# The low-part products of a sublayer's first two weight blocks, tile by tile for both blocks

## The chip, the cores and the metric

The kernel runs on one core of a Trainium2 chip. The metric is the device time of one execution, in microseconds. Before the change the median of three executions is 2408.03 us (2402.39 to 2408.96). About 0.3%, 7.2 us, is what a measurement of this kernel can tell from no change.

## The reference, cut to what matters

Two layers (DEPTH = 2) act on 544 token columns: 512 of a new stream and 32 of a running one. A layer is a half-step SwiGLU network, a mixer (latent attention beside retention) and a second half-step SwiGLU network, three sublayers in all:

```
h = modulated_pre(x, norm_pre[l, 0], mods, 0)      # rms_norm(x, g) * (1 + scale) + shift
x = gated_post(x, swiglu(h, w1, w3, w2), norm_post[l, 0], mods, 0, 0.5)
h = modulated_pre(x, norm_pre[l, 1], mods, 1)
o, st = mixer(h, l)                                # begins with z = h @ w_in
x = gated_post(x, o, norm_post[l, 1], mods, 1, 1.0)
h = modulated_pre(x, norm_pre[l, 2], mods, 2)
x = gated_post(x, swiglu(h, ...), norm_post[l, 2], mods, 2, 0.5)
```

Everything is float32. The model width is 1024 (8 tiles of 128 features), the hidden width 2816.

## The kernel before, in words

Activations lie feature-major: `x[:, k, :]` holds features 128k to 128k+127 on the partitions and the 544 tokens along the free axis. A matrix product in float32 accuracy is made of three products in the faster fp32r type: each operand is split into a high part (rounded to fp32r) and a low part (what is left), and high x high, high x low and low x high are added up in PSUM. `tile3` (L583, L584, L587) does this for one 128x128 weight tile, in two halves of the tokens.

Weights are streamed in chunks: a chunk is the column of 8 weight tiles that makes one output tile. SyncE loads chunk c into `raw[:, c % 2]`, ScalarE rounds it into `w_hi` (`high`, L1029, or `high_at`, L1036), GpSimd writes the rest into `w_lo` (`low`, L486), and TensorE multiplies. There are two slots of each. `high` of chunk c+2 waits on the semaphore `w_used` until TensorE has used chunk c, since both lie in one slot; `low` of c+2 waits for `high` of c+2, and TensorE's next block waits for `lo_done` of its chunk.

The change is in `first_tiles`, which makes the first two output tiles of each sublayer, chunks 0 and 1 (`w` = 0, 1) together, because the input h is only being made at that time. It runs six times. Its first loop goes over the 8 input tiles k, waits for `h_hi` of tile k (ScalarE, L1059) and adds `w_hi` x `h_hi` and `w_lo` x `h_hi` for both chunks (L621, L623). Its second part adds `w_hi` x `h_lo` (L631); `h_lo` is made by VectorE, two instructions a tile (L1413), the larger of 512 columns and a smaller of 32. Before the change it goes first through all k for chunk 0, waiting for `h_lo` of tile k, and after each second tile issues `pre_sum` (L593): products of a matrix of ones with squares of x, for the mean square of each token. A `pre_sum` or the `early_sum` after them shows as four matmul records. After chunk 0's last tile `w_used` is raised (slot 0 is free), then come `pre_sum` of the last square, `early_sum`, all 16 products of chunk 1, and the second `w_used`.

Then TensorE goes to the next block: chunk 2 by `feature(0, 1, 0)` in a SwiGLU sublayer or `z_tile(2, 4, 0)` in the mixer. It begins by waiting for `lo_done` of chunk 2, and its first matmul is an L583.

ScalarE's order at this place is written out in `pre_scale`: the squares (L1069), of which tile 6 waits for the first `pre_sum` and tile 7 for the second; then `high` of chunk 2, which waits for the first `w_used`; then the square root of the mean (L1039), which waits for `early_sum`; then `high` of chunk 3, which waits for the second `w_used`. GpSimd's order in `turn_over` is: `low` of chunks 0 and 1, the odd tiles of the new x, the sum of the first four squares (L503, L506), `low` of chunks 2 and 3. VectorE goes from `h_lo` to the reciprocal of the root (L1417) and then reads the finished output tiles.

Of the kernel before, what the change touches and what calls it, by code (L numbers as in the profile page):

```python
# [35 lines left out]
KD = D // P  # L36
# [71 lines left out]
def streaming_trunk(nc, a, o):  # L108
    ctx = ExitStack()
    with ctx:  # L110
# [24 lines left out]
        def signal(name, per_layer, before=0):  # L135
            return Signal(ctx.enter_context(nc.semaphore(name)), per_layer, before)
# [125 lines left out]
        w_used = signal("w_used", CH, 2)  # L262
# [15 lines left out]
        h_ready = signal("h_ready", 54)  # L278
        H_AT = (0, 18, 36)
# [290 lines left out]
        def _(pe):  # L570
# [19 lines left out]
            def add_squares(src, bank, start, stop, mat):  # L590

                for t in range(2):
                    last = pe.matmul(ps[:, bank + t, 0:HT], mat[:, :], src[:, t * HT:(t + 1) * HT],  # L593
                                     start=start, stop=stop)
                return last
# [16 lines left out]
            def first_tiles(l, j, chunk):  # L612

                for k in range(KD):
                    pe.wait_ge(h_high.sem, h_high.at(l, H_AT[j] + 2 + 2 * k + 2))
                    for w in range(2):
                        if k == 0:
                            pe.wait_ge(lo_done.sem, lo_done.at(l, chunk + w + 1))
                        for t, w_t in enumerate((HT, HB)):
                            n = slice(t * HT, t * HT + w_t)  # L620
                            pe.matmul(ps[:, 2 * w + t, 0:w_t], w_hi[:, w, k * P:(k + 1) * P], h_hi[:, k, n],  # L621
                                      start=k == 0, stop=False)
                            pe.matmul(ps[:, 2 * w + t, 0:w_t], w_lo[:, w, k * P:(k + 1) * P], h_hi[:, k, n],  # L623
                                      start=False, stop=False)
                for w in range(2):
                    for k in range(KD):
                        if w == 0:
                            pe.wait_ge(h_ready.sem, h_ready.at(l, H_AT[j] + 2 + 2 * k + 2))
                        for t, w_t in enumerate((HT, HB)):
                            n = slice(t * HT, t * HT + w_t)  # L630
                            last = pe.matmul(ps[:, 2 * w + t, 0:w_t], w_hi[:, w, k * P:(k + 1) * P], h_lo[:, k, n],  # L631
                                             start=False, stop=k == KD - 1)
                        if w == 0 and k % 2:
                            if k == KD - 1:
                                last.then_inc(w_used.sem, 1)
                            pre_sum(l, j, 4 + k // 2)
                    if w == 0:
                        early_sum(l, j)
                last.then_inc(w_used.sem, 1)

            def pre_sum(l, j, m):
                pe.wait_ge(x_sq.sem, x_sq.at(l, j * KD + m + 1))
                add_squares(tmp_s[:, m % 2, :], 6, m == N_EARLY, False, ones).then_inc(sums.sem, 1)

            def early_sum(l, j):
                pe.wait_ge(sq_added.sem, sq_added.at(l, j * SQ + N_EARLY))
                add_squares(squares[:, :], 6, False, True, ones).then_inc(sums.sem, 1)

            def up(l, s):

                base = FFN_C[s]

                def feature(i, f, w):
                    pe.wait_ge(lo_done.sem, lo_done.at(l, base + i * 4 + 2 * f + w + 1))
                    for k in range(KD):
                        last = tile3(4 * f + 2 * w, w, k, h_hi[:, k, :], h_lo[:, k, :], k == 0, k == KD - 1, HB)
                    last.then_inc(w_used.sem, 1)

                pe.wait_ge(up_out.sem, up_out.at(l, 2 * s * FT))
                first_tiles(l, 2 * s, base)  # L660
                feature(0, 1, 0)
                pe.wait_ge(rooted.sem, rooted.at(l, 4 * s + 1))
                feature(0, 1, 1)
                with pe.Fori(1, FT // 2) as i:
                    for f in range(2):

                        pe.wait_ge(up_out.sem, up_out.at(l, 2 * s * FT + i * 4 + 2 * f - 2))
                        for w in range(2):
                            feature(i, f, w)
# [43 lines left out]
            def mixer(l):  # L713
# [10 lines left out]
                def norm_sum(n, buf, bank, start, stop, mat=ones):  # L724
                    pe.wait_ge(m_sq.sem, m_sq.at(l, n + 1))
                    add_squares(tmp_s[:, buf, :], bank, start, stop, mat).then_inc(m_sum.sem, 1)

                first_tiles(l, 1, MIX_C0)
                z_tile(2, 4, 0)
                z_tile(3, 2, 1, 2)  # L730
# [1099 lines left out]
```

## Time and profile before

| what | us |
|---|---|
| median of 3 executions | 2408.03 |
| lowest and highest | 2402.39, 2408.96 |
| the profiled execution, its own time | 2406.11 |
| the profiled execution, span of its instructions | 2404.3 |
| TensorE busy | 2283.5 (95%) |
| TensorE loading weights | 2161.0 (90%) |
| VectorE busy | 1275.7 (53%) |
| GpSimd busy | 910.3 (38%) |
| ScalarE busy | 806.6 (34%) |

A busy TensorE is a stream of pipelined matmuls whose ends are modelled, so the distance from one start to the next tells its pace, not the length of a record.

### The profile page before, as it was taken

What the parts mean: (1) busy time and instruction counts of PE and PEld (TensorE: products, weight loads), DVE (VectorE), ACT (ScalarE), POOL (GpSimd) and SP (SyncE); (2) the same over time, 40 slices, a digit from 0 to 9 for tenths busy, and PEclk for the clock granted to TensorE, in tenths of its full rate; (3) what the DMA queues carried; (4) which work ended last, traced back from release to release, by engine and by line L of the source; (5) the groups of instructions that cost most, each with busy time, mean ns of one, the idle gap of its engine ahead of it and who ended that gap; (6) DMA issues with size and microseconds to landing.
All of it is one profiled execution on the core that took longest, in us unless ns stands there. A gap on an engine that the chain in (4) does not pass through costs nothing.

```text
span 2404.3 us, 44025 instructions
## 1 busy us (share of the span) xinstructions
PE 2283.5 (95%) x17536; PEld 2161.0 (90%) x17536; DVE 1275.7 (53%) x2099; ACT 806.6 (34%) x1329; POOL 910.3 (38%) x400
## 2 busy tenths in 40 slices
PE   1999999999999999999999999999998999999997
PEld 1999999899647899999989999998994599999997
DVE  7433369969362433337243333897856515333561
ACT  1422232343434422233242222324243544222321
POOL 1433334443211533334443334444331154333353
PEclk9999999999989999999999999999999999999998
DMA  6222258622210122226412222873231022222551
GB/s 237 71 87 87 87 192 277 217 71 79 89 36 27 62 88 87 87 94 242 145 53 88 87 87 86 286 275 110 88 109 49 2 71 71 87 87 87 190 197 71
DMA packets 72806, 273.06 MB, mean 114 GB/s; under 512 B 8784, under 2 KB 10192, under 8 KB 71952
## 3 DMA queue, kind: packets, MB, share of 16 engines
q1 hardware_dynamic: 72720, 271.88, 33.1%
q8 instruction: 58, 0.95, 0.2%
q14 instruction: 28, 0.23, 0.0%
HBM read 268.40 MB, written 3.45 MB: 113 GB/s over the span
## 4 chain that ended last, share of the span: by engine, by line
PE 67%; issue 17%; DVE 9%; POOL 2%; ACT 2%; DMA 1%; DVEq 0%; POOLq 0%; SPq 0%; ACTq 0%
PE ps L587 19%; PE ps L583 19%; PE ps L584 19%; POOL w_lo L486 2%; DVE wide_v L1353 2%; DMA ada_w<-in_ada 1%; PE ps L593 1%; PE ps L631 1%; DVE wide_v L1394 1%; PE ps L949 1%; PE ps L922 1%; PE ps L916 1%; PE ps L973 1%; DVE ret_root L1576 1%; DVE x L1398 1%
## 5 line engine op out<-in xcount | busy, mean ns | idle before, releaser
L486 POOL TENSOR_TENSOR w_lo<-raw,w_hi 128x1024 fp32r<-128x1024 f32 (+1 forms) x304 | 786.0, 2586 | 1342.0 <-ACT w_hi L1036 970.9
L583 PE MATMUL ps<-h_hi,w_hi 128*128 128x272 f32 x3296 | 886.8, 289 | 3.8 <-POOL w_lo L486 3.8
L584 PE MATMUL ps<-h_lo,w_hi 128*128 128x272 f32 x3296 | 889.4, 287 | 0.0
L587 PE MATMUL ps<-h_hi,w_lo 128*128 128x272 f32 x3296 | 685.7, 289 | 0.0
L583 PEld LDWEIGHTS ps<-h_hi,w_hi 128*128 128x128 f32 x3296 | 619.1, 188 | 5.3 <-POOL w_lo L486 5.1
L584 PEld LDWEIGHTS ps<-h_lo,w_hi 128*128 128x128 f32 x3296 | 620.9, 188 | 0.2
L1036 ACT CAST w_hi<-raw 128x1024 fp32r<-128x1024 f32 (+1 forms) x236 | 268.8, 1139 | 832.0 <-PE ps L587 761.4
L587 PEld LDWEIGHTS ps<-h_hi,w_lo 128*128 128x128 f32 x3296 | 519.1, 188 | 0.0
L583 PE MATMUL ps<-u_hi,w_hi 128*128 128x272 f32 x1408 | 380.9, 288 | 3.9 <-POOL w_lo L486 3.9
L584 PE MATMUL ps<-u_lo,w_hi 128*128 128x272 f32 x1408 | 380.1, 288 | 0.0
L1353 DVE CUSTOM_DVE_ANT_0 wide_v<-ada_w,ps 128x1024 bf16<-128x1024 f32 x288 | 332.3, 1217 | 46.3 <-DMA ada_w<-in_ada 28.9
L1431 DVE TENSOR_TENSOR wide_v<-ps,rinv 128x544 f32<-128x544 f32 x88 | 63.8, 724 | 437.3 <-PE ps L587 437.3
L587 PE MATMUL ps<-u_hi,w_lo 128*128 128x272 f32 x1408 | 291.8, 288 | 0.0
L583 PEld LDWEIGHTS ps<-u_hi,w_hi 128*128 128x128 f32 x1408 | 265.1, 188 | 4.7 <-POOL w_lo L486 4.7
L584 PEld LDWEIGHTS ps<-u_lo,w_hi 128*128 128x128 f32 x1408 | 264.9, 188 | 0.0
L1436 DVE SCALAR_TENSOR_TENSOR wide_v<-wide_v,wide_s 128x512 f32<-128x512 f32 (+1 forms) x176 | 193.9, 1140 | 104.8 <-ACT wide_s L1092 104.8
L587 PEld LDWEIGHTS ps<-u_hi,w_lo 128*128 128x128 f32 x1408 | 220.1, 188 | 0.0
L621 PE MATMUL ps<-h_hi,w_hi 128*128 128x272 f32 x192 | 63.1, 351 | 69.9 <-ACT h_hi L1059 61.2
L1095 ACT CAST u_hi<-wide_v 128x544 f32 (+1 forms) x88 | 57.0, 647 | 213.8 <-DVE wide_v L1436 213.8
L1029 ACT CAST w_hi<-raw 128x1024 fp32r<-128x1024 f32 x68 | 71.1, 1045 | 166.9 <-PE ps L587 88.1
L621 PEld LDWEIGHTS ps<-h_hi,w_hi 128*128 128x128 f32 x192 | 44.6, 232 | 74.7 <-issue 60.0
L1387 DVE RECIPROCAL tok_inv<-tok_root 128x5 f32<-128x5 f32 x6 | 1.1, 188 | 204.8 <-ACT tok_root L1043 204.8
(241 smaller groups left out, 2417.5 us busy)
## 6 DMA issues: line engine op xcount, KB each, us to landing
raw<-in_w_up SPq DMA_DIRECT2D x176, 512.0 KB, 3.3
ada_w<-in_ada SPq DMA_DIRECT2D x160, 512.0 KB, 4.7
raw<-in_w_dn SPq DMA_DIRECT2D x64, 704.0 KB, 5.5
raw<-in_w_mix SPq DMA_DIRECT2D x64, 512.0 KB, 3.3
decay<-in_decay SPq DMA_DIRECT2D x2, 2048.0 KB, 9.2
x<-in_x SPq DMA_DIRECT2D x1, 2176.0 KB, 9.0
rope_tab<-in_rope SPq DMA_DIRECT2D x2, 1088.0 KB, 4.8
out_y<-x SPq DMA_DIRECT2D x8, 272.0 KB, 2.1
```

The source lines that it names most:

```text
L486: pool.tensor_tensor(w_lo[:, slot, 0:width], raw[:, slot, 0:width], w_hi[:, slot, 0:width].bitcast(F32), ALU.subtract).then_inc(lo_done.se ...
L583: pe.matmul(ps[:, bank + t, 0:width[t]], wh, hi[:, n], start=start, stop=False)
L584: pe.matmul(ps[:, bank + t, 0:width[t]], wh, lo[:, n], start=False, stop=False)
L587: last = pe.matmul(ps[:, bank + t, 0:width[t]], wl, hi[:, n], start=False, stop=stop)
L593: last = pe.matmul(ps[:, bank + t, 0:HT], mat[:, :], src[:, t * HT:(t + 1) * HT], start=start, stop=stop)
L621: pe.matmul(ps[:, 2 * w + t, 0:w_t], w_hi[:, w, k * P:(k + 1) * P], h_hi[:, k, n], start=k == 0, stop=False)
L1029: nc.scalar.copy(w_hi[:, slot, 0:width], raw[:, slot, 0:width]).then_inc(hi_done.sem, 1)
L1036: nc.scalar.copy(w_hi[:, k, 0:width], raw[:, k, 0:width]).then_inc(hi_done.sem, 1)
L1095: nc.scalar.copy(u_hi[:, bass.ds(i * 2 + f, 1), :].rearrange("p a n -> p (a n)"), tmp_v[:, f, :]).then_inc(up_hi.sem, 1)
L1353: v_.tensor_tensor_reduce(junk[v], ada_w[:, t, :], c_row, 1.0, 0.0, ALU.mult, ALU.add, acc[:, v, t:t + 1]).then_inc(ada_done.sem, 1)
L1431: v_.tensor_tensor(halves(tmp_v[:, f, :]), pair(4 * f + 2), halves(rinv[:, :]), ALU.mult)
L1436: v_.scalar_tensor_tensor(out=wide_v[:, f, at], in0=wide_v[:, f, at], scalar=wide_v[:, f, T + 2 * v:T + 2 * v + 1], in1=wide_s[:, f, at], ...
```

## The change

In `first_tiles` the two loops of the low part are swapped: k outside, w inside. The products of chunk 1 with tile k of `h_lo` run right behind those of chunk 0 with the same tile, as in the high part. `pre_sum` comes after both chunks' products of each odd tile, and `early_sum` after everything. `w_used` is raised twice, by the last product of chunk 0 and by the last product of chunk 1, which now stand two matmuls apart. The number of instructions and of waits is the same.

```
-                for w in range(2):
-                    for k in range(KD):
-                        if w == 0:
-                            pe.wait_ge(h_ready.sem, h_ready.at(l, H_AT[j] + 2 + 2 * k + 2))
+                for k in range(KD):
+                    pe.wait_ge(h_ready.sem, h_ready.at(l, H_AT[j] + 2 + 2 * k + 2))
+                    for w in range(2):
                         for t, w_t in enumerate((HT, HB)):
                             n = slice(t * HT, t * HT + w_t)
                             last = pe.matmul(ps[:, 2 * w + t, 0:w_t], w_hi[:, w, k * P:(k + 1) * P], h_lo[:, k, n],
                                              start=False, stop=k == KD - 1)
-                        if w == 0 and k % 2:
-                            if k == KD - 1:
-                                last.then_inc(w_used.sem, 1)
-                            pre_sum(l, j, 4 + k // 2)
-                    if w == 0:
-                        early_sum(l, j)
-                last.then_inc(w_used.sem, 1)
+                        if k == KD - 1:
+                            last.then_inc(w_used.sem, 1)
+                    if k % 2:
+                        pre_sum(l, j, 4 + k // 2)
+                early_sum(l, j)
```

## Rows read from the trace of the kernel before

**Rows 1.** The page: the chain that ended last, by engine.

```profile
PE 67%; issue 17%; DVE 9%; POOL 2%; ACT 2%; DMA 1%; DVEq 0%; POOLq 0%; SPq 0%; ACTq 0%
```

**Rows 2.** The chain in order of time, 480 to 500: start, us, what.

```profile
488.81 0.74 PE ps L631 x4
...
489.58 1.06 ACT w_hi L1029
...
490.70 2.38 POOL w_lo L486
```

**Rows 3.** Low part by stretch, L631 alone: length, PE (x count), PEld, clock, DMA.

```profile
483.47:493.23 9.76, 6.44 (x32) 4.67 (x32) 1.00 0.00 0
...
65.69:74.31 8.62, 5.49 (x32) 4.49 (x32) 1.00 0.01 2
```

**Rows 4.** Timeline, TensorE, first sublayer: start, us, what, [idle before].

```profile
65.69 0.67 PE L631 MATMUL ps<-h_lo,w_hi 128*128 128x272 f32 x4
...
69.75 0.86 PE L631 MATMUL ps<-h_lo,w_hi 128*128 128x272 f32 x4
70.46 1.08 PE L593 MATMUL ps<-wide_s,ones 128*128 128x272 f32 x4
...
72.09 2.38 PE L631 MATMUL ps<-h_lo,w_hi 128*128 128x272 f32 x16
74.31 0.31 PE L583 MATMUL ps<-h_hi,w_hi 128*128 128x272 f32 x1
```

**Rows 5.** Timeline, ScalarE and GpSimd, first sublayer.

```profile
70.66 1.05 ACT L1029 CAST w_hi<-raw 128x1024 fp32r<-128x1024 f32 x1 [1.26 <-PE ps L631]
...
71.78 2.39 POOL L486 TENSOR_TENSOR w_lo<-raw,w_hi 128x1024 fp32r<-128x1024 f32 x1 [6.39 <-ACT w_hi L1029]
```

**Rows 6.** Timeline, TensorE, second sublayer.

```profile
484.07 0.52 PE L631 MATMUL ps<-h_lo,w_hi 128*128 128x272 f32 x2 [0.19 <-DVE h_lo L1413]
...
488.45 1.09 PE L631 MATMUL ps<-h_lo,w_hi 128*128 128x272 f32 x4
...
493.23 0.31 PE L583 MATMUL ps<-h_hi,w_hi 128*128 128x272 f32 x1
```

**Rows 7.** Timeline, ScalarE, GpSimd and VectorE, second sublayer.

```profile
489.58 1.05 ACT L1029 CAST w_hi<-raw 128x1024 fp32r<-128x1024 f32 x1 [1.72 <-PE ps L631]
491.41 0.72 ACT L1039 ACTIVATE root<-ps,eps 128x544 f32<-128x544 f32 x1 [0.79 <-PE ps L593]
...
490.70 2.38 POOL L486 TENSOR_TENSOR w_lo<-raw,w_hi 128x1024 fp32r<-128x1024 f32 x1 [6.74 <-ACT w_hi L1029]
...
482.67 6.30 DVE L1413 SCALAR_TENSOR_TENSOR h_lo<-x,mul_pre,h_hi 128x32 fp32r<-128x32 f32 x13
```

**Rows 8.** Timeline, third sublayer, behind the first tiles: TensorE, then ScalarE.

```profile
831.96 0.31 PE L583 MATMUL ps<-h_hi,w_hi 128*128 128x272 f32 x1
...
844.12 0.29 PE L583 MATMUL ps<-h_hi,w_hi 128*128 128x272 f32 x1
...
837.55 0.65 ACT L1095 CAST u_hi<-wide_v 128x544 fp32r<-128x544 f32 x1 [1.07 <-DVE wide_v L1436]
838.27 1.05 ACT L1036 CAST w_hi<-raw 128x1024 fp32r<-128x1024 f32 x1
```

**Rows 9.** Timeline, TensorE: idle gaps elsewhere, in a mixer.

```profile
588.34 0.39 PE L583 MATMUL ps<-h_hi,w_hi 128*128 128x272 f32 x1 [1.21 <-POOL w_lo L486]
...
650.00 0.74 PE L835 MATMUL ps<-ret_q,ret_k 64*128 64x256 f32 x4 [1.85 <-DVE ret_st L1569]
662.26 0.70 PE L835 MATMUL ps<-ret_q,ret_k 64*128 64x256 f32 x4 [1.79 <-DVE ret_st L1569]
```

**Rows 10.** Stretches round those gaps: length, PE, PEld, DVE, ACT, POOL, clock, DMA.

```profile
584.00:592.00 8.00, 6.79 (x54) 6.57 (x54) 7.94 (x9) 4.58 (x7) 5.18 (x2) 1.00 0.20 66
...
651.00:654.00 3.00, 3.00 (x9) 1.06 (x8) 2.15 (x3) 0.00 (x0) 0.00 (x0) 0.51 0.00 0
...
662.00:665.00 3.00, 2.74 (x13) 1.21 (x14) 1.62 (x3) 0.00 (x0) 0.00 (x0) 1.00 0.00 0
```

## The prediction

> **What bounds the kernel now.** I read the chain of waits first, since the change moves only the order of TensorE's work. TensorE is 67% of the chain that ended last, against 9% VectorE and 2% each GpSimd and ScalarE [rows 1]: the reader is to see that a microsecond of new TensorE idleness is a microsecond of the kernel, wherever no later wait swallows it. Then I read the chain around the second sublayer's first tiles, in order of time. There it leaves TensorE: low products to 489.55, the cast of chunk 2 (489.58), its low part on GpSimd (490.70, 2.38 us) and back to TensorE [rows 2]. So what ends last at this place is the conversion of the next weights, which begins when the first `w_used` frees slot 0, and exactly this release is moved by the change. Third, the stretches of the low part: from its first product to the next block's first, 8.62 us in the first sublayer and 9.76 us in the second [rows 3]; the other four are of that second kind (9.76 or 9.77 us), so there are five of it. Fourth, the timelines of both kinds [rows 4 to 7].
>
> **Pace.** Let p be the time of one low product and s that of one of the 20 records of `pre_sum` and `early_sum`. In the first sublayer TensorE waits for nothing: 16p + 8s = 74.31 - 70.46 = 3.85 us and 32p + 20s = 74.31 - 65.69 = 8.62 us [rows 4]. Hence s = 0.23 and p = 0.126 us. In the five others the same work takes 9.76 us, 1.14 us more, lost to waits for `h_lo` during chunk 0's products: a tile of `h_lo` costs VectorE some 0.97 us (6.30 us for 13 instructions, two a tile), and in that loop it is asked for faster than that [rows 6, 7].
>
> **What is added and removed.** No instruction comes or goes, and the waits are as many as before. Three things move.
>
> *The release of slot 0.* Before, chunk 0's last product follows 15 other products and 12 sum records; after, 29 products and the same 12. That is 14p = 1.76 us later, where nothing waits. In the first sublayer it was at 69.75 + 0.86 = 70.61 [rows 4], so it comes at 72.37.
>
> *The waits for `h_lo`.* With both chunks a tile keeps TensorE for 4p = 0.50 us, and every second tile for 0.92 us more: 0.96 us a tile, about VectorE's pace. VectorE finishes the last tile at 488.97 [rows 7]. In the new order the last tile's first product is due at 483.47 + 28p + 12s = 489.76, so the margin is 0.8 us. One short wait stays, for the second tile: its first product ran at 484.07 [rows 6] and would be due at 483.97, so 0.10 us. The release in the second sublayer was at 488.45 + 1.09 = 489.54, that is 6.07 us behind the first product; it comes at 483.47 + 29p + 12s + 0.10 + 0.28 (the modelled length behind a start, from the first sublayer's 70.61 against 65.69 + 15p + 12s) = 490.26. The shift is 0.72 us: 1.76 us less 1.04 us of waits that go.
>
> *What covers the conversion.* From the release to the end of GpSimd's work it is 74.17 - 70.61 = 3.56 us in the first sublayer [rows 5] and 493.08 - 489.54 = 3.54 us in the second [rows 7]. Before, TensorE had 16p + 8s = 3.85 us of work behind the release, so the conversion was just hidden. After, it has 2p + 8s = 2.09 us. The cover is gone and the conversion becomes the wait.
>
> **The sum.** The next block starts when GpSimd is done, plus a start delay for which I take 0.05 us (from both sides: not under 0, and not over the 0.14 us from GpSimd's end to the block's start in [rows 4, 5], where TensorE was still busy). First sublayer: 72.37 + 3.56 + 0.05 = 75.98 against 74.31, +1.67 us. Second: 490.26 + 3.54 + 0.05 = 493.85 against 493.23, +0.62 us, and the same in four more. Together 1.67 + 5 x 0.62 = 4.8 us. TensorE should stand idle for about 1.5 us in front of the next block, in all six.
>
> **What else hangs on it.** `early_sum` ends later by 0.96 us in the five (2.02 us, less 1.06 us of waits; the root at 491.41 waited for it [rows 7]), and so do the root, the reciprocal and the reading of the first output tile. TensorE asks for the result of that only after two further blocks, 844.12 - 831.96 = 12.2 us later [rows 8]. The cast of chunk 4 (838.27) stands behind VectorE's and ScalarE's work on the first tile (until 838.20): it would move to about 839.2, its GpSimd part ends about 3.5 us later at 842.7, and it is wanted at 844.7, so 2 us are left. The cast of chunk 3 no longer waits for the second `w_used` and comes right behind the root, a little earlier than before. SyncE's loads into `raw` wait for GpSimd and move by the same 0.6 to 1.7 us, queued ahead of nothing that is wanted within 5 us. All these are costed at nothing; if the margin of 2 us were gone, each microsecond missing would be paid up to six times. Behind the first tiles the whole program moves rigidly, since each later stage starts from TensorE. The sum against the profiled execution is 2406.1 + 4.8 = 2410.9 us; that execution lies 1.9 us under the median, and on the median it is 2408.0 + 4.8 = 2412.8 us.
>
> **The rivals.**
>
> *Slower still: the new gap drops TensorE's clock.* After an idle time of 1.85 us before 650.00 the granted clock was 0.51 in 651 to 654, that is 1.2 GHz; after 1.79 us before 662.26 it stayed 1.00, and after 1.21 us before 588.34 too [rows 9, 10]. A gap of 1.5 us lies between. What speaks against: TensorE does dense work on both sides of it, unlike at 650. A fall that covers 3 us costs half of it in work not done, 1.5 us. In all six: 4.8 + 9 = 13.8 us, 2421.8 us; from two falls on (7.8 us) it passes 0.3%. The Trainium skill (TensorE: Matmul & The Clock Gate, "A second HAM failure mode: psum-queue depth-cycling") tells that short idle times between groups of matmuls, repeated often, bring the clock down and cost throughput. By it the result would be this rival's; the trace has one gap with and two without a fall, so it is not decided. Chance 0.19.
>
> *Not slower: the conversion does not bind.* If `lo_done` of chunk 2 came early enough (a cast or GpSimd part shorter by 1.5 us at this place), only the waits for `h_lo` would go: 5 x 1.04 = 5.2 us less, 2402.8 us. For it speaks only that 1.1 us is truly lost there in each of five sublayers. Against it, GpSimd's part took 2.38 and 2.39 us in both and the cast 1.05 us, and no order of TensorE shortens them. It decides from the point at which the conversion takes under 2.09 us. Chance 0.06.
>
> *The waits for `h_lo` do not go.* If VectorE still paced the low part (its tiles cost some 0.97 us, TensorE's 0.96 us), each of the six would pay up to the full 1.67 us: 10.0 us, 2418.0 us. Chance 0.07.
>
> **How the numbers follow.** Forecast 0.68, rivals 0.19, 0.06, 0.07. Predicted time 2412.8 us. The range is 2405 to 2422: its top takes in the clock rival in all six and the third, its foot leaves out most of the second and lets the medians scatter by 3 us (the runs before spread over 6.6 us). What a measurement can tell from no change is 7.2 us (0.3%); the forecast's 4.8 us lies inside, and a scatter of 2.4 us upward would carry it out, to which I give 0.05 of its 0.68. Slower by over 0.3%: the clock rival's cases of two or more falls (0.16), the third (0.06), the scatter: 0.27. Faster by over 0.3%: 0.03. Within: 0.70.
>
> **What would show it.** In the profile after: 16 product records between groups of sums become groups of eight; no idle time of L631 for `h_lo` but the one of 0.1 us; `w_used` to the cast still 0.04 us; before the first L583 behind each low part an idle time of about 1.5 us ended by GpSimd's `w_lo` L486, six times, where there is none now; the stretches of the low part 10.3 us in the first sublayer and 10.4 us in the others; ScalarE's wait for L631 at the second cast gone; the granted clock 1.00 through it. The prediction is wrong if that gap is missing or under 1 us, if waits for `h_lo` stay, if the clock falls within 4 us behind a gap, or if a later wait takes the delay up, so that the time is that of before.

## The result

The changed kernel is slower. Its median is 2417.4 us (2408.47 to 2419.82, 10 executions) against 2405.52 us for the kernel before (2398.54 to 2409.83, 10 executions); the ratio is 1.0046, 95% interval 1.0035 to 1.0057. A second comparison (e1 below) gave 1.0032 (1.0019 to 1.0045). The predicted time was 2412.8 us. The forecast had the right cause, and its 4.8 us are nearly what the changed place costs (5.2 us); the whole loss is larger, 11.9 us by these medians and 7.5 us by the second comparison's, and why is only in part shown below.

### The profile page after: what moved, and what is told of

Read it like the earlier page. It is cut to its first block, busy times and chain, and to the rows that moved or that the text cites. A ratio compares the mean times of both kernels' runs of the same rounds, so it can differ in the third digit from the quotient of the medians.

```text
span 2417.3 us, 44025 instructions
## 1 busy us (share of the span) xinstructions
PE 2289.5 (95%) x17536; PEld 2163.4 (89%) x17536; DVE 1273.8 (53%) x2099; ACT 805.3 (33%) x1329; POOL 909.6 (38%) x400
## 4 chain that ended last, share of the span: by engine, by line
PE 68%; issue 15%; DVE 7%; POOL 3%; ACT 3%; DMA 2%; DVEq 0%; POOLq 0%; SPq 0%; ACTq 0%
PE ps L587 19%; PE ps L583 19%; PE ps L584 19%; POOL w_lo L486 3%; DVE wide_v L1350 2%; DMA ada_w<-in_ada 2%; PE ps L919 1%; PE ps L913 1%; PE ps L946 1%; PE ps L630 1%; PE ps L970 1%; ACT h_hi L1056 1%; PE ps L593 1%; DVE acc L1350 1%; DVE wide_v L1391 1%
## 5 line engine op out<-in xcount | busy, mean ns | idle before, releaser
L1026 ACT CAST w_hi<-raw 128x1024 fp32r<-128x1024 f32 x68 | 70.9, 1043 | 164.4 <-PE ps L587 88.2
```

The lines of the kernel that those rows point to most:

```text
L1026: nc.scalar.copy(w_hi[:, slot, 0:width], raw[:, slot, 0:width]).then_inc(hi_done.sem, 1)
```

## The profile after

The profiled execution took 2419.1 us, its span is 2417.3 us, 13.0 us more than before. The low products are L630 now, and lines behind the edit are three lower (the cast is L1026, not L1029). The stretches of the low part come first, from its first product to the first product of the next block (length, PE and PEld busy time of L630 alone, clock, DMA share, GB/s):

```profile
66.09:76.32 10.23, 5.26 (x32) 4.34 (x32) 1.00 0.01 2
486.93:497.39 10.46, 5.50 (x32) 4.39 (x32) 1.00 0.00 0
...
2001.72:2012.23 10.51, 5.54 (x32) 4.43 (x32) 1.00 0.01 2
```

Against 8.62 and 9.76 us [rows 3] that is 1.61 us more in the first sublayer and 0.67 to 0.75 us more in the five others, 5.2 us in all (62.6 against 57.4 us, the six added up). TensorE's timeline in the first sublayer answers to [rows 4] (start, length, engine, line, what, and in brackets the idle time before it and who ended it):

```profile
66.09 1.17 PE L630 MATMUL ps<-h_lo,w_hi 128*128 128x272 f32 x8
67.10 1.08 PE L593 MATMUL ps<-wide_s,ones 128*128 128x272 f32 x4
...
71.65 1.36 PE L630 MATMUL ps<-h_lo,w_hi 128*128 128x272 f32 x8
72.86 1.08 PE L593 MATMUL ps<-wide_s,ones 128*128 128x272 f32 x4
73.77 1.08 PE L593 MATMUL ps<-squares,ones 128*128 128x272 f32 x4
76.32 0.39 PE L583 MATMUL ps<-h_hi,w_hi 128*128 128x272 f32 x1 [1.47 <-POOL w_lo L486]
```

The products come in groups of eight, the sums between them, and nothing but eight sum records stands behind the last product. Then TensorE is idle for 1.47 us until GpSimd's `w_lo` ends. ScalarE and GpSimd in the second sublayer answer to [rows 7]:

```profile
493.87 1.04 ACT L1026 CAST w_hi<-raw 128x1024 fp32r<-128x1024 f32 x1 [2.01 <-PE ps L630]
495.95 0.71 ACT L1036 ACTIVATE root<-ps,eps 128x544 f32<-128x544 f32 x1 [1.04 <-PE ps L593]
496.57 1.03 ACT L1026 CAST w_hi<-raw 128x1024 fp32r<-128x1024 f32 x1
...
494.99 2.34 POOL L486 TENSOR_TENSOR w_lo<-raw,w_hi 128x1024 fp32r<-128x1024 f32 x1 [7.55 <-ACT w_hi L1026]
```

The conversion itself is as long as before: 493.87 to 497.33 is 3.46 us, and was 3.50 us from the cast's start [rows 7]. It only begins later against TensorE's work. The cast of chunk 3 (496.57) now follows the root without a wait. The chain of waits has the same three steps as [rows 2], now as they stand here, and the block behind starts 0.06 us after the last of them:

```profile
493.09 0.76 PE ps L630 x6
...
493.87 1.05 ACT w_hi L1026
...
494.99 2.34 POOL w_lo L486
```

In the list of waits, TensorE's wait for `w_lo` is 17.1 us in 14 places (first line: who waited, for whom: us in total, times, longest); before it was 7.7 us in 8 places. The other two lines are of the view of L630. The idle time before the low products because of `h_lo` is 0.9 us in TensorE's two rows (matmul and weight load) together, where it was 5.7 us. ScalarE waited for these products in 6 places, where it did in 12: its wait at the second cast is gone, as forecast.

```profile
PE ps L583 <- POOL w_lo L486: 17.1, 14, 1.6
...
  DVE h_lo L1410: 0.9, 5
  ACT w_hi L1026: 12.1, 6
```

So 5.2 of the 13.0 us lie in the low parts. Of the other 7.8 us, 4.0 lie between the fifth low part and the sixth (327.7 us from block to next low part, 323.7 before), where the attention of the second layer is; the rest is spread over the other stretches, 1.4 us at most in one. Two windows of 35 us that begin at about the same point of the work there, first of the kernel before, then of the changed one (length, PE, PEld, DVE, ACT, POOL busy, clock, DMA share, GB/s):

```profile
1855.00:1890.00 35.00, 31.78 (x226) 18.33 (x222) 24.50 (x56) 19.32 (x51) 6.83 (x5) 0.90 0.18 61
```

```profile
1863.00:1898.00 35.00, 33.56 (x188) 18.14 (x186) 22.09 (x51) 16.51 (x44) 5.48 (x4) 0.71 0.17 61
```

The granted clock was 0.71 there against 0.90, and the changed kernel got through 188 matmul records where 226 were done before. The whole execution had 0.977 against 0.981. Between the fifth low part and the sixth the clock was at 1.2 GHz for 23.9 us, and for 10.2 us before. The profiles of the later runs show that this can come without the change: the same part took 329.2 us (27.3 us at 1.2 GHz) in e7, whose low parts are those of before, and 324.6 us (17.1 us at 1.2 GHz) in e1, which is the changed kernel again. Whether the change makes it more likely is the question that is left.

## The experiments

Each execution comes with its mean granted clock, and that explains most of the spread of one kernel: the 69 executions of the kernel before whose clock is on record (those beside e1 to e8) lie between 2397.85 us (clock 0.985) and 2412.93 us (0.977). I therefore fitted all executions with a recorded clock with one level for each row of the table and one slope for the clock. The slope is 1.7 us for each 0.001 of clock, and the scatter left is 1.2 us instead of 3.9. "At the same clock" below is the difference of levels from this fit, with its 95% interval; "low parts" is the sum of the six stretches in the kernel's profile less the 57.4 us of before. A difference at the same clock leaves out whatever a kernel loses by a lower clock of its own.

| kernel | ratio, 95% interval | low parts | at the same clock | mean clock |
|---|---|---|---|---|
| changed, first comparison | 1.0046 (1.0035, 1.0057) | +5.2 | +5.9 ± 0.8 | 0.9783 |
| e1 changed, again | 1.0032 (1.0019, 1.0045) | +5.2 | +4.9 ± 0.8 | 0.9797 |
| e2 late release | 1.0098 (1.0075, 1.0120) | +16.4 | +18.2 ± 1.0 | 0.9790 |
| e3 lag of four tiles | 1.0024 (1.0011, 1.0038) | +1.6 | +1.7 ± 0.8 | 0.9785 |
| e4 interleaved, split conversion | 0.9995 (0.9981, 1.0010) | -3.8 | -3.4 ± 0.8 | 0.9801 |
| e5 filler, no idle time | 1.0033 (1.0018, 1.0049) | +5.3 | +6.2 ± 0.8 | 0.9797 |
| e6 idle time only | 1.0052 (1.0034, 1.0071) | +11.1 | +12.2 ± 0.9 | 0.9806 |
| e7 before, split conversion | 0.9998 (0.9984, 1.0011) | 0.0 | 0.0 ± 0.8 | 0.9802 |
| e8 as e4, again | 0.9984 (0.9972, 0.9996) | -3.8 | -3.4 ± 0.8 | 0.9801 |
| before, 69 executions | | 0 | 0 | 0.9804 |

The mean clock of the kernel before was not the same in each comparison: 0.9810 beside e1 to e4, 0.9802 beside e5 to e7, 0.9796 beside e8. Single executions scatter by about 0.002, so the mean of 6 to 12 of them is known to 0.001 or 0.002. The ten executions of the kernel before in the first comparison have no clock on record, so the changed kernel's are set against the 69 others. e2, e5 and e6 lie 0.9 to 1.8 us over their low parts at the same clock, just beyond their intervals, and no row here says where.

**e1: the changed kernel again** (no edit).

> The changed kernel once more, to see how much of its loss is fixed and how much goes with the granted clock of each execution. Release theory (the loss at the first tiles is the conversion of chunk 2, uncovered since slot 0 is released later; 5.2 us in the profile after, the rest is clock time elsewhere that has nothing to do with the change): idle time of about 1.5 us before the block behind each of the six low parts, and a median 5 to 7 us over before in this call. Gap theory (the six new idle times bring the clock down more often, so that the loss is fixed at some 11 us): median 10 to 12 us over before, and low-clock stretches that begin within some 4 us behind the gaps or are longer at the next ones.

Measured: median 2413.53 us (12 executions) against 2406.04, so 7.5 us, just above the band of the release theory (5 to 7 us, missed by 0.5 us) and under that of the gap theory. All six idle times are 1.47 or 1.48 us, and again no low clock begins behind one. At the same clock the loss is 4.9 us, what the low parts show.

**e2: the release alone, later.** In the order of before:

```
                        if w == 0 and k % 2:
-                            if k == KD - 1:
-                                last.then_inc(w_used.sem, 1)
                             pre_sum(l, j, 4 + k // 2)
+                        if w == 1 and k == 3:
+                            last.then_inc(w_used.sem, 1)
```

> The order of before (all of chunk 0, sums, all of chunk 1), but slot 0's release is raised by chunk 1's product of tile 3 instead of chunk 0's last. Only the release moves, by 8 sum records and 8 products: 1.84 + 1.01 = 2.85 us. Release theory: the block behind starts 2.7 us later in each of the six, idle time about 2.7 us each, 16.4 us over before, with the waits for h_lo as before. Order theory (the interleaving of both chunks' products itself is what costs): no change against before. Gap theory: 16.4 us and at least 6 us more for the clock, 22 us or more.

Measured: low parts of 11.33 and 12.46 to 12.51 us, 2.7 us each more than before, as forecast, and 16.4 us in all. Nothing is interleaved here, so the order theory is out: the release alone makes a loss of this kind. The median is 2426.28 us against 2406.04, 20.2 us, between the release theory's 16.4 and the gap theory's 22 or more: here the clock does fall at the idle time. TensorE's timeline at the first one, and the four stretches of the profile in which the clock was low at a block's start (they begin between about 0.5 us before it and 1 us after; columns as above):

```profile
71.91 2.38 PE L631 MATMUL ps<-h_lo,w_hi 128*128 128x272 f32 x16
76.84 0.59 PE L583 MATMUL ps<-h_hi,w_hi 128*128 128x272 f32 x1 [2.55 <-POOL w_lo L486]
77.23 0.43 PE L584 MATMUL ps<-h_lo,w_hi 128*128 128x272 f32 x1
77.46 0.43 PE L583 MATMUL ps<-h_hi,w_hi 128*128 128x276 f32 x1
```

```profile
76.30:79.70 3.40, 2.86 (x12) 2.86 (x13) 3.28 (x1) 2.31 (x3) 2.78 (x2) 0.50 0.43 154
1253.90:1257.30 3.40, 3.40 (x17) 3.40 (x17) 2.75 (x6) 0.94 (x2) 1.75 (x1) 0.50 0.64 184
1677.20:1680.60 3.40, 3.40 (x17) 3.40 (x16) 2.71 (x6) 1.33 (x3) 1.29 (x1) 0.50 0.67 224
2011.70:2015.10 3.40, 2.85 (x12) 2.85 (x13) 3.13 (x4) 0.96 (x2) 2.82 (x2) 0.50 0.44 154
```

From 77.23 on the products start every 0.23 us, not every 0.126: 1.2 GHz. At idle times of 2.55 to 2.57 us the clock fell in four of six places, at those of 1.47 to 1.57 us in none of six in the changed kernel's profile, in none of six in e1 and in none of six in e6.

**e3: chunk 1 four tiles behind chunk 0.**

```
-                for k in range(KD):
-                    pe.wait_ge(h_ready.sem, h_ready.at(l, H_AT[j] + 2 + 2 * k + 2))
-                    for w in range(2):
+                lag = 4
+                for step in range(KD + lag):
+                    for w, k in ((0, step), (1, step - lag)):
+                        if not 0 <= k < KD:
+                            continue
+                        if w == 0:
+                            pe.wait_ge(h_ready.sem, h_ready.at(l, H_AT[j] + 2 + 2 * k + 2))
...
-                    if k % 2:
-                        pre_sum(l, j, 4 + k // 2)
+                    if step < KD and step % 2:
+                        pre_sum(l, j, 4 + step // 2)
```

> Interleaved as in the change, but chunk 1 stays four tiles behind chunk 0, so the release comes behind 24 products instead of 30 (before: 16), and chunk 1's products fill some of the waits for h_lo. Release theory: in the first sublayer the release is 1.0 us later and the next block 0.9 us; in the five others the release is about 0.2 us later and the next block 0.1 us: 1.3 us over before in all, not to be told from it. Order theory: as slow as the change, since eight of each chunk's products still alternate in halves: 5 us or more.

Measured: low parts of 9.27 and 9.93 to 9.96 us, 0.65 and some 0.2 us over before, and an idle time of 0.48 us each; 1.6 us in all against 1.3 forecast. The split between the places was forecast a little wrong, the sum nearly right. The medians do not bear the forecast out: 2413.43 us against 2406.04 is 7.4 us, as much as e1's 7.5 and within what the order theory said (5 us or more), and the ratio of 1.0024 can be told from 1. At the same clock it is 1.7 us, so the rest goes with the clock: 0.9785 against 0.9810 of the kernel before beside it, a difference of 0.0025 ± 0.0012. This profile was at 1.2 GHz for 51 us in the attention of both layers, as the changed kernel's was, with a third of its idle time.

**e4: the change, with the conversion of chunk 2 in two halves.** GpSimd and TensorE are edited in the same way as ScalarE, whose lines stand here; TensorE's next block waits for `lo_half` at tile 0 and for `lo_done` at tile 4.

```
-                high(l, next_chunk + 2, 0, KD * P)
+                h, c = KD * P // 2, next_chunk + 2
+                act.wait_ge(w_used.sem, w_used.at(l, c - 1))
+                act.wait_ge(landed[0].sem, landed[0].at(l, 16 * (c // 2) + 16))
+                nc.scalar.copy(w_hi[:, 0, 0:h], raw[:, 0, 0:h]).then_inc(hi_half.sem, 1)
+                nc.scalar.copy(w_hi[:, 0, h:2 * h], raw[:, 0, h:2 * h]).then_inc(hi_done.sem, 1)
```

> The changed kernel with the conversion of chunk 2 cut in two at tile 4 on ScalarE and GpSimd, so that the next block can start when the first half is ready, about 1.9 us behind the release instead of 3.6. Release theory: the idle times of 1.5 us go; what is left of the change is the 1.1 us of waits for h_lo that it fills in five sublayers: the low part takes 8.6 to 8.7 us in the first and 8.9 us in the others (before 8.62 and 9.76), so 4.3 us under before and 9 to 10 us under the changed kernel. Order theory: still over before. Gap theory: as the release theory, and the clock part of the loss goes too.

Measured: low parts of 8.73 and 8.96 to 9.00 us, no idle time; median 2405.19 us against 2406.04, where 4.3 us less were forecast, and 8.3 us under the changed kernel's 2413.53 beside it. This comparison alone cannot tell it from before; at the same clock it is 3.4 us less. The order theory, by which it would still be over before, is out. In the second sublayer (ScalarE, GpSimd, TensorE):

```profile
489.94 0.62 ACT L1094 CAST w_hi<-raw 128x512 fp32r<-128x512 f32 x1 [2.01 <-PE ps L638]
...
490.63 1.27 POOL L527 TENSOR_TENSOR w_lo<-raw,w_hi 128x512 fp32r<-128x512 f32 x1 [7.11 <-ACT w_hi L1094]
...
490.90 1.08 PE L601 MATMUL ps<-squares,ones 128*128 128x272 f32 x4
491.95 0.39 PE L591 MATMUL ps<-h_hi,w_hi 128*128 128x272 f32 x1
```

The first half is ready 1.96 us after the cast began (491.90), TensorE is then just done with its sums, and the block starts at 491.95. With the conversion out of the way the interleaved order shows what it is good for: the waits for `h_lo` are filled, 0.8 us in each of five places.

**e5: as much delay as the change makes, without idle time.** In the order of before:

```
                     if w == 0:
                         early_sum(l, j)
+                        for _ in range(7):
+                            pe.matmul(ps[:, 4, 0:HT], w_hi[:, 1, 0:P], h_lo[:, 0, 0:HT], start=True, stop=True)
```

> The order of before with seven products more behind early_sum in each of the six first tiles (into a PSUM bank that the next block overwrites), so TensorE has 7 x 0.126 = 0.88 us more work and no idle time: the block behind starts 0.85 us later, 5.1 to 5.3 us in all, as much as the changed kernel loses at that place. Release theory: 5.1 to 5.3 us over before, and the mean granted clock of its executions that of before (0.981). Gap theory: the same here, against 7 to 11 us with the gaps. Delay theory (any later start of the stages behind, dense or idle, costs more than itself through the clock): as much as the changed kernel, 7 us or more, and a mean granted clock of 0.979 to 0.980.

Measured: 5.3 us more in the low parts, TensorE dense, and 2415.0 us against 2407.57: 7.4 us, as in e1, without any new idle time. The forecast of the release theory (5.1 to 5.3 us in the whole time) failed as it did in e1, and the numbers of the delay theory (7 us or more, 0.979 to 0.980) came: the mean clock is 0.9797. That does not show the delay theory, since the kernel before had 0.9802 beside it, which is no difference clear of the scatter; 6.2 ± 0.8 us of the loss stand at the same clock. e6 delays the same stages by twice as much, and its clock is not lower.

**e6: the idle time without the interleaving.** In the order of before slot 0 is released by one product behind `early_sum`:

```
-                            if k == KD - 1:
-                                last.then_inc(w_used.sem, 1)
...
                     if w == 0:
-                        early_sum(l, j)
+                        early_sum(l, j).then_inc(w_used.sem, 1)
...
+                return pe.matmul(ps[:, 4, 0:HT], w_hi[:, 1, 0:P], h_lo[:, 0, 0:HT], start=True, stop=True)
```

> The order of before, but slot 0 is released behind early_sum (by one product put there for it) instead of behind chunk 0's last product: 8 sum records and one product later, 1.97 us. TensorE is left with 16 products, 2.0 us, to cover a conversion of 3.6 us, so it stands idle for the same 1.5 us as in the change, with nothing interleaved and the waits for h_lo as before. Release theory: the low part takes 10.6 us in the first sublayer and 11.7 us in the others, 11.8 us over before at the same granted clock. Gap theory: besides, the clock falls more often than in the kernel with filler: 15 us or more over before. Order theory: no change.

Measured: low parts of 10.45 and 11.61 to 11.63 us, idle times of 1.56 us, 11.1 us in all; median 2417.68 us against 2407.57, 10.1 us, and 12.2 us at the same clock. The release theory's 11.8 us came, the order theory's none and the gap theory's 15 or more did not. Its mean clock, 0.9806, is the highest of the table (0.9802 for the kernel before beside it), with six idle times as long as the change's. TensorE's timeline in the first sublayer:

```profile
70.94 0.49 PE L646 MATMUL ps<-h_lo,w_hi 128*128 128x272 f32 x1
71.27 2.17 PE L631 MATMUL ps<-h_lo,w_hi 128*128 128x272 f32 x16
75.00 0.39 PE L583 MATMUL ps<-h_hi,w_hi 128*128 128x272 f32 x1 [1.56 <-POOL w_lo L486]
```

**e7: the split conversion in the order of before** (the edit of e4 on the kernel before).

> The order of before with the conversion of chunk 2 cut in two at tile 4, the other half of the kernel with both. Release theory: in the order of before TensorE's own work (3.85 us) already covers the conversion, so a shorter one gains nothing: low parts of 8.6 and 9.7 us, 0 to 0.5 us under before. If instead cutting it in two brings something of its own (the cast of chunk 3 comes earlier or later, GpSimd is free earlier), it would be 3 us or more under before, and the gain of the kernel with both would be none of the interleaving's.

Measured: low parts of 8.61 and 9.75 to 9.77 us, exactly before's, and a ratio of 0.9998. A shorter conversion alone gains nothing, interleaving alone loses 5.2 us, both together gain 3.8 us at that place.

**e8: e4 once more** (no edit to it).

> The kernel with the interleaved order and the split conversion once more, since its first comparison could not tell it from before. Release theory: low parts of 8.7 and 9.0 us again, 3.8 us less than before in all, and at the same mean granted clock 3 to 4 us under before. If its median is not under that of before in this call either, the gain is real at the first tiles but too small to be told in the whole kernel's time.

Measured: median 2403.26 us against 2410.25, ratio 0.9984 (0.9972 to 0.9996). At the same clock both comparisons put it 3.4 us under before. The medians are 0.9 and 7.0 us under, and the ratios 0.05 and 0.16%, of which only the second is clear of 1: the version is faster than before by little, and clearly faster than the changed kernel.

## Why the prediction was right, and where it was not

*What bounds the place: right, and shown.* The forecast took the conversion of chunk 2, from the release of slot 0 to `w_lo`, as what ends last. e2 moved only the release and e6 the release with one product added (0.13 us), and they paid 2.7 and 1.8 to 1.9 us at each place; e4 only cut the conversion in two, so that its first half is ready sooner, and the idle times went.

*Pace, release, cover: right to 0.1 us.* The first cast comes 6.71 us after the first low product in the first sublayer (6.72 forecast) and 6.94 us in the second (6.83 forecast). What was missed is that the wait for the second tile of `h_lo` also costs the product behind it: the starts are 487.31, 487.55, 487.78 and 487.91, so a step of 0.23 us where 0.126 was taken. The start delay of 0.05 us and the idle time of "about 1.5 us" (1.47) came as written. The sum was 10.29 and 10.38 us for a low part; measured 10.23 and 10.44 to 10.51. In all 5.2 us, forecast 4.8.

*What else hangs on it, costed at nothing: right for the waits.* The root, the cast of chunk 4 and the mixer's chain caused no new wait. In a down projection one wait of TensorE for `w_lo` was 1.58 us (at 365.04) where it was 1.06 us before; in e1, the same kernel, it is 1.06 us again, so it is not tied to the change. The statement that all behind moves rigidly holds for the order of the work and not for its clock.

*Where the size was off: the sum was taken for the whole loss.* The two comparisons of the changed kernel lie 11.9 and 7.5 us over before in their medians; over 22 against 69 executions the means differ by 7.7 ± 1.9 us. At the same clock it is 5.9 and 4.9 us, the term that the prediction sized. The rest, 2 to 3 us on average, goes with a mean clock of 0.979 against 0.9804, and most of the low clock that differs from one profile to the next lies in the attention stages.

*The total: inside the range, in part by luck.* 2417.4 us lies between 2405 and 2422, but the top of that range was drawn for the clock rival and the third rival, and neither came. The forecast itself was 4.8 us more and put the result most likely within 0.3% of before (0.70); the first comparison is clear of 0.3%, the second lies around it.

*The clock rival: wrong in its mechanism.* I gave it 0.19 with a clock that falls behind each new idle time. In 18 idle times of 1.47 to 1.57 us (three profiles) it fell behind none; e6, with the same idle times, had the highest clock, and e5, with none, had e1's clock and e1's loss. The Trainium skill (TensorE: Matmul & The Clock Gate, "A second HAM failure mode: psum-queue depth-cycling") tells of short idle times between groups of matmuls, frequent enough to bring the clock down again and again. This case's traces do not show that at idle times of 1.47 to 1.57 us, six in an execution; at e2's of 2.56 us the clock fell in four of six. Whether the lower mean clock of the changed kernel is caused by the change stays open. For a cause speaks that both its comparisons and e3's are low (0.9783, 0.9797 and 0.9785, where the kernel before had 0.9810 beside e1 and e3); against it, that e4 and e8, e5, e6 and e7 lie within 0.001 of the kernel before beside them, interleaved, delayed, idle or none of these. No run tells which property of the order would do it. The chance of 0.27 for slower by over 0.3% was too low for that reason: with 5 us of fixed loss, a clock lower by 0.001 to 0.002 is enough to pass 0.3%.

*The rival that the conversion does not bind* failed as a forecast of the change and is what e4 built: 5.2 us less was its price, 3.8 us came in the low parts. In the five sublayers in which TensorE waits, the wait for the second tile of `h_lo` and its slow restart stay; in the first, 8.73 us were taken against 8.62.

*The rival that the waits for `h_lo` stay: wrong.* Five waits are left, one in each of the five sublayers as forecast, 0.9 us in both of TensorE's rows together, against 25 waits and 5.7 us.

## What to carry to other kernels

An order of products that looks better for one input (each `h_lo` tile used twice as it arrives) can be worse for the buffer that they free: ask first which instruction releases the slot of the next weights, how long their conversion takes, and how much work stands behind that release. Idle time inside a block is worth filling only if what stands behind the release is still longer than the refill, or the refill is cut so that its first part is enough. When runs of one kernel spread with the granted clock, compare kernels at the same clock before a story is told about the rest.

## What the runs showed of the hardware

The mean granted clock of a whole execution lay between 0.977 and 0.985 for the kernel before and between 0.976 and 0.984 for the changed one, and the time moved with it by 1.7 us for each 0.001. In the attention stages of both layers the time at 1.2 GHz added up to 14 us in the profile of e2 and to 51 us in that of e7, whose low parts are before's to 0.02 us. At TensorE's idle times of 2.55 to 2.57 us (e2) the clock was down for 3.4 us in four of six cases, and at 18 of 1.47 to 1.57 us in none. These lie between dense work; in the attention of the kernel before, a fall followed an idle time of 1.85 us [rows 9, 10], so the length alone does not decide. The first product after a short wait for `h_lo` was followed by the next after 0.23 us and not 0.126 us, at the full clock (487.55 to 487.78 in the changed kernel).
